# Products with the values in two attentions of a single-core block: values held fixed, a pair's turned weights moved, two heads in two halves of the array's columns

## What is computed

```python
def causal_block_attention(q, k, v, log_decay=None):     # fox: with log_decay; mla: without
    def step(args):
        qc, i = args[0], args[1]
        logits = jnp.einsum('bhqd,bhkd->bhqk', qc, k).astype(jnp.float32)
        ...
        logits = jnp.where(key_idx[None, :] <= q_idx[:, None], logits, -jnp.inf)
        p = jax.nn.softmax(logits, axis=-1).astype(v.dtype)
        return jnp.einsum('bhqk,bhkd->bhqd', p, v)
```

## Time and profile before

| | |
|---|---|
| median of 3 runs | 1582.45 us (1582.36 to 1582.68) |
| span of the profiled execution | 1580.1 us |
| time of an execution that lies around the span (median less span) | 2.35 us |
| TensorE busy | 1545.3 us (98%) |
| VectorE / ScalarE / GpSimd busy | 824.7 / 736.3 / 322.4 us |
| fox attention, pure part | about 494 to 576 us of the span |
| mla attention | about 1037 to 1161 us of the span |

### The profile page before, as it was taken

One profiled execution on the slowest core, in us unless ns is written; L12 is line 12 of the kernel. 1 busy time (PEld: TensorE's weight loads), 2 busy tenths in 40 slices (PEclk: granted clock), 3 DMA queues, 4 the chain that ended last, 5 costly groups with the idle time before them and its releaser, 6 DMA issues. The chain is left out here.

```text
span 1580.1 us, 22237 instructions
## 1 busy us (share of the span) xinstructions
PE 1545.3 (98%) x9054; PEld 1299.5 (82%) x9054; DVE 824.7 (52%) x1406; ACT 736.3 (47%) x1423; POOL 322.4 (20%) x273
## 2 busy tenths in 40 slices
PE   7999998999999999999999999999999999999999
PEld 6788787998898887788888888768887888888887
DVE  5355456556435755745334543668955644244442
ACT  4355445455654545544124443567845534133431
POOL 0000142001430001244013431032001343014420
PEclk9999999999999999999999999999999999999999
DMA  6202112323220103233223332110013333223331
GB/s 232 80 35 88 54 54 88 129 68 107 80 88 30 33 1 104 81 110 118 85 82 102 99 110 72 51 44 14 15 54 93 94 94 123 90 80 94 110 116 41
DMA packets 37462, 128.07 MB, mean 81 GB/s; under 512 B 4192, under 2 KB 8944, under 8 KB 37360
## 3 DMA queue, kind: packets, MB, share of 16 engines
q1 hardware_dynamic: 37360, 126.65, 25.3%
HBM read 124.54 MB, written 2.10 MB: 80 GB/s over the span
## 5 line engine op out<-in xcount | busy, mean ns | idle before, releaser
L321 PE MATMUL bank<-hhi,whi 128*128 128x512 f32 (+2 forms) x1064 | 419.4, 394 | 4.8 <-ACT hhi L1915 3.0
L323 PE MATMUL bank<-hhi,wlo 128*128 128x512 f32 (+2 forms) x1064 | 415.0, 390 | 0.0
L322 PE MATMUL bank<-hlo,whi 128*128 128x512 f32 (+2 forms) x1064 | 414.9, 390 | 0.0
L312 DVE TENSOR_TENSOR wlo<-wstage,whi 128x1024 fp32r<-128x1024 f32 (+9 forms) x250 | 278.6, 1117 | 129.4 <-ACT whi L302 129.0
L302 ACT CAST whi<-wstage 128x1024 fp32r<-128x1024 f32 (+9 forms) x250 | 236.1, 949 | 135.9 <-PE bank L323 131.2
L321 PEld LDWEIGHTS bank<-hhi,whi 128*128 128x128 f32 (+2 forms) x1064 | 199.2, 187 | 53.0 <-ACT hhi L1915 6.3
L2414 DVE SCALAR_TENSOR_TENSOR cr<-bank,vc,cr 128x511 f32<-128x511 f32 (+1 forms) x168 | 125.9, 749 | 217.1 <-ACT cr L2353 214.1
L323 PEld LDWEIGHTS bank<-hhi,wlo 128*128 128x128 f32 (+2 forms) x1064 | 199.0, 187 | 43.6
L322 PEld LDWEIGHTS bank<-hlo,whi 128*128 128x128 f32 (+2 forms) x1064 | 199.1, 187 | 41.4 <-issue 0.5
L2353 ACT ACTIVATE cr<-bank,vc 128x512 f32<-128x512 f32 x84 | 65.5, 780 | 248.5 <-PE bank L323 248.5
L2459 POOL TENSOR_TENSOR cr<-cr,cr 128x512 f32<-128x512 f32 x44 | 94.4, 2146 | 314.5 <-DVE cr L2414 279.8
(11 more groups left out here) (423 smaller groups left out, 2343.5 us busy)
## 6 DMA issues: line engine op xcount, KB each, us to landing
wstage<-in_wts SPq DMA_DIRECT2D x147, 512.0 KB, 3.6
wstage<-in_wts SPq DMA_DIRECT2D x32, 704.0 KB, 4.1
wstage<-in_wts SPq DMA_DIRECT2D x14, 768.0 KB, 4.3
xT<-in_x SPq DMA_DIRECT2D x4, 512.0 KB, 5.0
xt<-in_x SPq DMA_DIRECT2D x4, 512.0 KB, 6.6
out<-ob SPq DMA_DIRECT2D x8, 256.0 KB, 2.3
U<-in_rel_ext SPq DMA_DIRECT2D x6, 256.0 KB, 9.0
wstage<-in_wts SPq DMA_DIRECT2D x2, 603.0 KB, 3.8
```

Source lines behind the costliest of these rows:

```text
L312: e.tensor_tensor(K.wlo[i % 3][:, p], K.stage[i % 3][:, p], K.whi[i % 3][:, p].bitcast(F32), SUB).then_inc(*K.dve.up(("wlo", i) if last el ...
L321: e.matmul(o, lh, rh, start=start, stop=False)
L322: e.matmul(o, lh, rl, start=False, stop=False)
L323: return e.matmul(o, ll, rh, start=False, stop=stop)
```

## The change

In fox and mla the products with the values are no longer made item by item. When a pair's last item (in fox's memory pairs, the last item of tiles 0 and 1, then of 2 and 3) has been turned, PE makes all its products in one lump: the fixed operand is a block of values (128 keys x 64), the moving one the turned weights of up to four query tiles (up to 512 columns), and head s of the pair writes partitions 64s to 64s+63 of the bank. The result is already turned (head width on the partitions), so `y` needs no turning. The reciprocals of the row sums do: POOL spreads them over 64 columns a head (`pool_att`), PE turns that (`factors`), ACT copies it to SBUF, and DVE multiplies the bank by it in one instruction. ACT and DVE then split `y` from SBUF. The turned weights go to buffers that hold a whole pair (10 blocks a head), where the blocks of one key block lie side by side; the copy of a tile of four blocks takes two instructions. The stage has one step more at its end. The first block's band attention is not touched.

```diff
@@ class Attention
+        self.steps = range(-2, len(self.items) + (9 if lumps else 8))
+        if lumps:
+            self.item_at = {item: t for t, item in enumerate(self.items)}
+            self.lump_end = {max(self.lump_items(p, n)): (p, n) for p in range(len(heads) // 2) for n in range(len(lumps(p)))}
...
     def post(self, t):
-        return self.done(t - 7) if self.gen else None
+        return self.done(t - 8) if self.gen else None
@@ def pe_att
+    def lump(p, part):
...
+        for t in sorted(A.lump_items(p, part)):
+            q.wait_ge(*K.at((A.name, "pt", t)))
+        keys = A.n(A.item_at[2 * p, tiles[-1]]) // P
+        for j in range(keys):
+            for s in range(2):
...
+                z = e.matmul(b[64 * s:64 * s + 64, i0 * P:(i0 + n) * P], H.v(j), A.turned(A.item_at[2 * p, i0])[A.name, "pt", p, part][s][:, at:at + n, :],
+                             start=j == 0, stop=j == keys - 1)
...
+    def factors(p):
+        b = A.T.take(q, (A.name, "R", p))
+        q.wait_ge(*K.at((A.name, "rr over", p)))
+        for i in range(4):
+            z = e.transpose(b[:, i * P:(i + 1) * P], A.y[A.name, "y", p][:, i * P:(i + 1) * P], K.ident[:])
...
-        if 5 <= t <= N + 4:
+        if A.lumps is None and 5 <= t <= N + 4:
             pv(t - 5)
-        p = A.post(t)
-        if p is not None:
-            q.wait_ge(*K.at((A.name, "fin", p)))
-            b = A.T.take(q, (A.name, "yT", p))
-            for c in range(4):
-                z = e.transpose(b[:, c * P:(c + 1) * P], A.y[A.name, "y", p][:, c, :], K.ident[:])
-            z.then_inc(*K.pe.up((A.name, "yT", p), frees=[(A.name, "y", p)]))
+        if A.lumps and t - 5 in A.lump_end:
+            lump(*A.lump_end[t - 5])
+        if A.lumps and A.done(t - 5) is not None:
+            factors(A.done(t - 5))
@@ def act_att
+        p = A.done(t - 6) if A.lumps else None
+        if p is not None:
+            act_evac(e, q, K, (A.name, "factors", p), (A.name, "R", p), A.y[A.name, "y", p][:], K.bank((A.name, "R", p))[:])
         p = A.post(t)
...
-            act_hi(e, q, K, (A.gen, "hi", kt), (A.name, "yT", p), K.hhi[:, kt, :])
+            e.copy(K.hhi[:, kt, :], A.y[A.name, "y", p][:]).then_inc(*K.act.up((A.gen, "hi", kt)))
+def pool_att(e, q, K, A):
+    for t in A.steps:
+        p = A.done(t - 3)
...
+            e.tensor_copy(y[:].rearrange("p (i h n) -> p h i n", i=4, h=2),
+                          A.rs[:, 2 * p:2 * p + 2, :].unsqueeze(3).to_broadcast([P, 2, 4, 64])).then_inc(*K.pool.up((A.name, "rr over", p)))
@@ def dve_att
+        p = A.done(t - 3) if A.lumps else None
...
+            e.reciprocal(rr, rr).then_inc(*K.dve.up((A.name, "rr", p)))
+        p = A.done(t - 7) if A.lumps else None
...
+            e.tensor_tensor(y[:], K.bank((A.name, "O", p))[:], y[:], MUL).then_inc(
+                *K.dve.up((A.name, "fin", p), frees=[(A.name, "O", p)]))
...
+                for j0, part, at in A.blocks(t - 3):
+                    z = e.tensor_copy(o[:, at, :], b[:, j0 * P:(j0 + len(part)) * P].rearrange("p (j n) -> p j n", j=len(part)))
...
-            if A.done(t - wait) is not None:
+            if A.lumps is None and A.done(t - wait) is not None:
                 finish(A.done(t - wait), tiles)
@@ def schedule
-    out += ["out0"] + ["foxatt"] * 3 + ["out0"] * 7 + ["bar5"] + ["norm1"] * 2 + ["ffn0"] * 63 + ["bar6"] + ["norm2"] * 2
+    out += ["out0"] + ["foxatt"] * 4 + ["out0"] * 7 + ["bar5"] + ["norm1"] * 2 + ["ffn0"] * 63 + ["bar6"] + ["norm2"] * 2
```

More of the change, by code:

```diff
@@ L1010, in __init__, with lump_items, lump_of, block @@
         self.last = [max(t for t, item in enumerate(self.items) if item[0] // 2 == p) for p in range(len(heads) // 2)]
-        self.given, self.pta = given, pta
-        self.steps = range(-2, len(self.items) + 8)
+        self.given, self.pta, self.lumps = given, pta, lumps
+        self.steps = range(-2, len(self.items) + (9 if lumps else 8))
+        if lumps:
+            self.item_at = {item: t for t, item in enumerate(self.items)}
+            self.lump_end = {max(self.lump_items(p, n)): (p, n) for p in range(len(heads) // 2) for n in range(len(lumps(p)))}
+            self.lump_begin = {min(self.lump_items(p, n)): (p, n) for p, n in self.lump_end.values()}
+    def lump_items(self, p, n):
+        return [self.item_at[2 * p + s, i] for s in range(2) for i in self.lumps(p)[n]]
+    def lump_of(self, t):
+        h, i = self.items[t]
+        return h // 2, [i in tiles for tiles in self.lumps(h // 2)].index(True)
+    def block(self, t, j):
+        h, i = self.items[t]
+        if self.heads[h].width(0) == P:
+            return (0, 4, 8, 7)[j] + i - j
+        tiles = self.lumps(h // 2)[self.lump_of(t)[1]]
+        return len(tiles) * j + i - tiles[0]
     def n(self, t):
@@ L1033, in done, with blocks, turned @@
         return self.last.index(t) if t in self.last else None
+    def blocks(self, t):
+        at = [self.block(t, j) for j in range(self.n(t) // P)]
+        split = 3 if at == [3, 6, 9, 7] else len(at)
+        return [(j0, part, slice(part[0], part[-1] + 1, part[1] - part[0] if len(part) > 1 else 1))
+                for j0, part in ((0, at[0:split]), (split, at[split:])) if part]
+    def turned(self, t):
+        return (self.pt if self.pta is None or self.items[t][0] >= 4 else self.pta)
     def turned_on_act(self, t):
@@ L1079, in turn @@
         z.then_inc(*K.pe.up((A.name, "T", t), frees=[(A.name, "P", t)]))
+    def lump(p, part):
+        tiles = A.lumps(p)[part]
+        if part == 0:
+            A.O.go_on_at(A.out_bank(p))
+            A.O.take(q, (A.name, "O", p))
+        b = K.bank((A.name, "O", p))
+        for t in sorted(A.lump_items(p, part)):
[3 more added lines that the diff above has]
+            for s in range(2):
+                H = A.heads[2 * p + s]
+                for r in H.v_ready(j):
+                    q.wait_ge(*K.at(r))
+                i0 = max(j, tiles[0]) if H.width(0) == P else tiles[0]
+                n = tiles[-1] + 1 - i0
+                at = A.block(A.item_at[2 * p + s, i0], j)
+                z = e.matmul(b[64 * s:64 * s + 64, i0 * P:(i0 + n) * P], H.v(j), A.turned(A.item_at[2 * p, i0])[A.name, "pt", p, part][s][:, at:at + n, :],
+                             start=j == 0, stop=j == keys - 1)
+        last = part == len(A.lumps(p)) - 1
+        z.then_inc(*K.pe.up(*[(A.name, "pv", p)] * last, frees=[(A.name, "pt", p, part)]))
+    def factors(p):
[3 more added lines that the diff above has]
+            z = e.transpose(b[:, i * P:(i + 1) * P], A.y[A.name, "y", p][:, i * P:(i + 1) * P], K.ident[:])
+        z.then_inc(*K.pe.up((A.name, "R", p)))
     def pv(t):
@@ L1122, in pe_att, with turned_tile @@
         yield
+def turned_tile(q, A, t):
+    p, part = A.lump_of(t)
+    if t in A.lump_begin:
+        A.turned(t).take(q, (A.name, "pt", p, part))
+    return A.turned(t)[A.name, "pt", p, part][A.items[t][0] % 2]
 def act_att(e, q, K, A):
@@ L1149, in act_att @@
             n = A.n(t - 3)
-            o = (A.pt if A.pta is None else A.pta).take(q, (A.name, "pt", t - 3))
-            act_evac(e, q, K, (A.name, "pt", t - 3), (A.name, "T", t - 3), o[:, 0:n], K.bank((A.name, "T", t - 3))[:, 0:n])
+            if A.lumps is None:
+                o = A.pt.take(q, (A.name, "pt", t - 3))
+                act_evac(e, q, K, (A.name, "pt", t - 3), (A.name, "T", t - 3), o[:, 0:n], K.bank((A.name, "T", t - 3))[:, 0:n])
+            else:
+                o, b = turned_tile(q, A, t - 3), K.bank((A.name, "T", t - 3))
+                q.wait_ge(*K.at((A.name, "T", t - 3)))
+                for j0, part, at in A.blocks(t - 3):
+                    z = e.copy(o[:, at, :], b[:, j0 * P:(j0 + len(part)) * P].rearrange("p (j n) -> p j n", j=len(part)))
+                z.then_inc(*K.act.up((A.name, "pt", t - 3), frees=[(A.name, "T", t - 3)]))
         if A.prep(t):
@@ L3094, in memory @@
         keys0 = sb("kt0", [P, 4, 4, 96], scope=s)
-    sb("parts", [P, 16, T])
+    K.parts = sb("parts", [P, 16, T])
     K.xT = sb("xT", [P, 8, T])
@@ L3187, in memory @@
     K.ff = [feed_forward(0)]
+    with above(0) as s:
+        seventh = Buffer(K, [sb("mla_seventh0", [P, 10, P], scope=s)], [(("mq", 7), "T"), (("mk", 7), "T")])
+        sb("below_seventh", [P, 256], scope=s)
+        seventh.t = (*seventh.t, sb("mla_seventh1", [P, 10, P], scope=s))
     with ExitStack() as s:
```

82 lines of the change are left out of this document (57 added, 25 removed).

## The result

The changed kernel takes 1609.62 us (median of 4 runs, 1604.81 to 1612.96) beside 1582.4 us for the kernel before: ratio 1.0181, 95% interval 1.0159 to 1.0202, so it is 27 us **slower**. The forecast was 1564 us, 18 us faster, with a range of 1554 to 1578: both are wrong. The profiled execution of the changed kernel took 1604.81 us, span 1603.1, 23 us over the span before.

A forecast was written before the change was run, and what follows sets the result against it. PE was taken to bound fox alone and late mla narrowly. Savings of 9 us in fox, 5.4 in late and 4 in early mla, 18.4 in all, cut the span from 1580.1 to 1561.7; with 2.35 around it, 1564 us, range 1554 to 1578.

The forecast's parts named there:

- Lump, 2.54 us a causal pair: PE's products: a causal pair's lump costs 2.54 us instead of 4.4, column halves side by side, some load time showing.
- rival of serial halves: Column halves run one after the other on PE, a causal pair costs 4.3 to 5.1 us: about 1591 us, chance 0.08.
- I leave 2 us for that: Fox: 2 us allowed for lumps coming in one piece while the score-to-turning loop has only three steps of slack.
- Three engines level in one loop ... I take 77.5: Late mla: PE 74, DVE 71.4, ACT 70.3 us do not reach the largest sum; 77.5 us taken, 6.5 saved.
- the first part, where I took 4 us: Early mla: PE's saving, the vanished 1.97 us bank wait and the low clock behind it offer 8 us; 4 taken.
- The four transposes of factors replace the four of y: nothing: PE in both attentions: the factors' transposes take the place of those of y, at no added cost.
- One or two more falls at 3.3 us each: A thinner PE load lowers the clock once or twice more, 3.3 us each; part of the 1575 us rival, chance 0.17.
- 1.1 us of idle time: End of each attention: PE idles 1.1 us between the last turning and the end of its copy.
- 25 us of PE saved: PE's net saving over both attentions, 12.2 us in fox and 13.0 in mla; all of it gained was a 0.08 rival.
- my fox term of 9: Fox: 12.2 us saved on PE less 3.1 for lumps and the end gives 9 us.
- mla terms of 5.4 and 4: Mla: late part 6.5 us less 1.1 for the end gives 5.4; early part 4 of 8 on offer.
- the loop sets the pace: PE idles between lumps, DVE and ACT near full: mla gives 3 us, fox 4, total 1575 us; chance 0.17.

The follow-up runs named there:

- e5: Changed kernel with every product of a lump made twice into the same sum: 1644.09 us, ratio 1.0389.
- e4: Changed kernel with every turning of the weights in fox and mla made twice: 1611.0 us, ratio 1.0202.
- e9: Changed kernel with only the first key block's products in each lump: 1590.54 us, ratio 1.0055.
- e6: Kernel before with only the first key block's product of each item, 88 of 152 products left out in each attention: 1563.19 us, ratio 0.9882.
- e13: Changed kernel without the factors' transposes and ACT's copy, the last product taking them untransposed: 1596.04 us, ratio 1.0085.
- e11: Changed kernel with each block of a turned tile copied by its own DVE instruction: 1620.47 us, ratio 1.025.
- e14: Changed kernel with first-key-block products only in lumps and without the factors' transposes and ACT copy: 1575.72 us, ratio 0.9976.
- e12: Changed kernel with mla's products one key block a step behind the scores, and factors copied first in ACT's step in both attentions: 1592.43 us, ratio 1.0066.

## Why the prediction was wrong

- **Lump, 2.54 us a causal pair: right, too high.** 2.1 us from first to last start, 2.3 to the next instruction (1131.62 to 1133.93). The rival of serial halves fell, at its deciding point: it wanted 1.7 times one half alone, and two take as long as one.
- **"I leave 2 us for that"** (fox, lumps in one piece). This step failed. It set an engine's total against another's and left a token for the burst. But the loop score, maximum, exponential, turning runs over PE each step; while PE is away, DVE eats its lead and stops (2.38 and 2.95 us idle behind the two lumps shown). So the lump is not paid out of PE's share but added to the loop: e5 shows 16 and 21 us for doubling it (where e4's turnings, as much PE work, cost 4 and 0), e9 gives back 17.9 for shortening it. Why the loop doesn't make the time up between lumps isn't shown.
- **"Three engines level in one loop ... I take 77.5"** (late mla). Failed with it. I had DVE at 86% and ACT at 80% of late mla and counted on 6.5 us; e6 shows 4.9 us for all of mla even for a saving of 19.4 us that adds nothing to the others. And the first part, where I took 4 us, is in it: the bank wait of 1.97 us went as foretold, but not the low clock behind it; 6.8 us at 1.2 GHz stood there before, and 6.8 stand between 1067 and 1085 after, where PE waits for ACT's exponentials instead (1.19 us at 1065.96).
- **"The four transposes of factors replace the four of y: nothing"** and ACT's copy inside its busy sum. Failed: leaving them out gives 11.5 us (e13). The new transposes come directly behind the lump, and hold one of two turning banks for ACT, which comes to them late. How much of the 11.5 is which isn't shown.
- **The clock.** One or two more falls at 3.3 us each were the rival's; it was 23.9 us more of low time in the attentions, at most 12 us. Here it comes behind a stretch in which PE is often idle, at the end of fox:

```profile
565.00:567.00 2.00, 1.12 (x8) 0.64 (x7) 2.00 (x5) 0.54 (x3) 0.00 (x0) 1.00 0.00 0
567.00:569.00 2.00, 0.63 (x4) 0.42 (x4) 1.71 (x4) 1.73 (x5) 0.00 (x0) 1.00 0.00 0
569.00:571.00 2.00, 1.11 (x4) 0.71 (x4) 1.56 (x6) 0.00 (x0) 0.61 (x1) 0.53 0.00 0
571.00:573.00 2.00, 1.65 (x4) 0.59 (x6) 0.20 (x2) 0.00 (x0) 0.00 (x0) 0.50 0.04 8
```

PE is busy for 1.12 and 0.63 of 2 us, then the clock is down, and the lump that follows takes nearly twice its length, 4.5 us instead of 2.3, with nothing beside it:

```profile
571.35 4.53 PE L1131 MATMUL bank<-fox_pt,fv 128*64 128x512 f32 x16 [0.94 <-DVE fox_pt L1320]
575.81 0.70 PE L1140 MATMUL bank<-ident,parts 128*128 128x128 f32 x4
576.27 0.48 PE L321 MATMUL bank<-hhi,whi 128*128 128x512 f32 x1
```

For this end I had 1.1 us of idle time, which was fair (0.94), and no low clock.
- **Room.** 25 us of PE saved were valued at 18.4; e6 says 17 for 39. The room that my fox term of 9 counted on was there (12.0 in e6, for more work taken off); the room for the mla terms of 5.4 and 4 was not.

The rival "the loop sets the pace" had the right sign of the mechanism and stopped at giving the saving back: 1575 us. It did not ask whether a loop that loses PE for one lump gets longer than it was. What the prediction named as signs against it, "if PE waits for factors or copies by more than 5 us an attention, or if the clock falls inside the attentions", both came, the first in mla alone (7.9 us).

Open: why one lump in fox leaves the clock higher than four pieces; how much of e11's price and of e14's distance to e6 is clock; how much of mla's distance to before in e12 (5.6 us) is the factors' way; and whether factors could do without a bank of the turning ring, which wasn't tried.

## What to carry to other kernels

Work taken off the busiest engine is worth only the lead that it has over the loop's other engines, and what that lead is can be measured by leaving the work out (e6: 17 us for 39). When an in-order engine serves a loop with little slack, ask for each piece of its other work how long those who wait for it can do without it: a rearrangement that halves the work but bundles it can cost the bundle's whole length (e5). Smaller pieces gave back 10 us in mla, 17 to 18 when they also stood behind the scores, and cost fox 10 to 12, so the piece size has to be tried in each place. And price a new small operation that borrows a buffer from the loop's ring by where it stands and how long it holds the buffer as well, not only by its own time.

## What the runs showed of the hardware

Two float32 products on two halves of the array's columns, both with all 128 rows, start 0.006 to 0.007 us apart at the full clock and take the time of one; 16 records with 16 loads of 64 columns start within 2.1 us. In the lines by shape of the changed kernel the records of a lump look slow, since the two halves overlap in time and low-clock lumps are in the mean (this group has 695 ns), while a turning has 293:

```profile
L1111 PE MATMUL bank<-ident,tmp 128*128 128x128 f32 x304 | 57.6, 293 | 17.1 <-ACT y L460 7.9 <-ACT tmp L1208 6.7 <-DVE fox_pt L1320 1.6
...
L1131 PE MATMUL bank<-fox_pt,fv 128*64 128x512 f32 x24 | 7.4, 695 | 0.9 <-DVE fox_pt L1320 0.9
```

And less work on PE can mean a lower clock: doubling the turnings alone (e4) took the low time in fox from 10.2 to 0 us and in mla from 20.5 to 6.8, and so gave back up to 5 of its 9 us in fox and 7 of 7 in mla. But the amount isn't what decides: e6 has 17 and 15 us less of PE's busy time than the kernel before and the same low time (0 and 6.8), and e9 has less than the changed kernel in both attentions and less low time too (6.8 and 13.7); by the test that its expectation set, thin PE work alone doesn't bring the clock down.
